# Keys and values of a second memory layer: from fillers inside a recurrent mixer to four joints between phases

## The reference, cut to what matters

```
def memory_cross_attention(h, mem, mem_kv_norm, mem_w_q, mem_w_kv, mem_w_o):
    q = (h @ mem_w_q)                       # 512 tokens, 4 heads of 128
    kv = rms_norm_2(mem, mem_kv_norm) @ mem_w_kv   # 256 tokens, 512 keys and 512 values
    k, v = kv[..., :512], kv[..., 512:]
    return block_attention(q, k, v, MEM_DIM ** -0.5) @ mem_w_o
```

## Time and profile before

| | us |
|---|---|
| median of three runs | 3618.82 (3618.14 to 3618.84) |
| the profiled execution | 3619.59 |
| its span on the core | 3617.6 |
| TensorE busy | 3500.1 (97%) |
| VectorE busy | 1948.1 (54%) |
| ScalarE busy | 1442.4 (40%) |
| mean granted TensorE clock | 0.992 |

### The profile page before, as it was taken

The page is one execution under the profiler, slowest core; times in us unless marked ns, Lnnn a source line. Parts: engine busy times, 40 slices in busy tenths (PEclk is TensorE's granted clock), DMA queues, the critical chain, the costliest instruction groups (busy, mean ns, idle before and its releaser), DMA issues.

```text
span 3617.6 us, 54110 instructions
## 1 busy us (share of the span) xinstructions
PE 3500.1 (97%) x21350; PEld 2891.6 (80%) x21350; DVE 1948.1 (54%) x2680; ACT 1442.4 (40%) x2153; POOL 29.3 (1%) x51
## 2 busy tenths in 40 slices
PE   8999998999999999999899999999999999999998
PEld 7888776768887888899678888877888897778887
DVE  4443489554434443335854433574777338567753
ACT  3333433143323332334643333573544236544432
POOL 0000000000000000000000000000000000000000
PEclk9999999999999999999999999999999999999999
DMA  3233222212232223322013233202232330123332
GB/s 129 97 105 107 93 71 82 75 64 98 93 97 83 94 98 95 92 82 89 23 59 98 95 96 93 66 13 70 82 99 96 94 107 18 47 70 99 99 95 92
DMA packets 85457, 303.41 MB, mean 84 GB/s; under 512 B 9712, under 2 KB 9712, under 8 KB 84400
## 3 DMA queue, kind: packets, MB, share of 16 engines
q1 hardware_dynamic: 82512, 288.24, 25.2%
q0 software_dynamic: 2784, 12.85, 1.0%
HBM read 294.76 MB, written 6.29 MB: 83 GB/s over the span
## 4 chain that ended last, share of the span: by engine, by line
PE 90%; DVE 6%; ACT 2%; issue 1%; DMA 0%; SPq 0%; DVEq 0%; ACTq 0%
PE PS L255 23%; PE PS L246 22%; PE PS L247 22%; PE PS L355 2%; PE PS L352 2%; PE PS L353 2%; PE PS L1065 2%; PE PS L1089 1%; PE PS L1076 1%; PE PS L386 1%; PE PS L2258 1%; DVE H_LO L479 1%; PE PS L2262 1%; ACT WHI L218 1%; DVE WLO L222 1%
## 5 line engine op out<-in xcount | busy, mean ns | idle before, releaser
L246 PE MATMUL PS<-WK_R,WHI 128*128 128x512 f32 x3648 | 1429.6, 392 | 16.8 <-DVE WLO L222 7.6
L247 PE MATMUL PS<-WK_R,WLO 128*128 128x512 f32 x3648 | 1423.7, 390 | 0.0
L222 DVE TENSOR_TENSOR WLO<-RAW,WHI 128x1024 fp32r<-128x1024 f32 x547 | 669.6, 1225 | 1150.1 <-ACT WHI L218 1147.4
L218 ACT ACTIVATE WHI<-RAW 128x1024 fp32r<-128x1024 f32 x547 | 579.4, 1059 | 998.6 <-PE PS L255 843.4
L246 PEld LDWEIGHTS PS<-WK_R,WHI 128*128 128x128 f32 x3648 | 687.5, 188 | 170.0 <-issue 22.3
L247 PEld LDWEIGHTS PS<-WK_R,WLO 128*128 128x128 f32 x3648 | 687.7, 189 | 142.6 <-issue 0.7
L255 PE MATMUL PS<-H_LO,WHI 128*128 128x512 f32 x2680 | 671.6, 391 | 3.9 <-DVE H_LO L479 3.9
L255 PEld LDWEIGHTS PS<-H_LO,WHI 128*128 128x128 f32 x2680 | 502.2, 188 | 115.9 <-DVE H_LO L479 13.1
L255 PE MATMUL PS<-HID_LO,WHI 128*128 128x512 f32 x1056 | 263.2, 389 | 0.0
L255 PEld LDWEIGHTS PS<-HID_LO,WHI 128*128 128x128 f32 x1056 | 197.9, 188 | 40.9
L1257 DVE SCALAR_TENSOR_TENSOR SC<-SC,VEC 128x511 f32<-128x511 f32 x176 | 132.2, 751 | 110.5 <-ACT SC L1224 98.6
(11 more groups left out here) (377 smaller groups left out, 3479.3 us busy)
## 6 DMA issues: line engine op xcount, KB each, us to landing
RAW<-in_ffn_gu SPq DMA_DIRECT2D x176, 512.0 KB, 3.5
RAW<-in_f_up SPq DMA_DIRECT2D x88, 512.0 KB, 3.6
RAW<-in_ffn_dn SPq DMA_DIRECT2D x64, 512.0 KB, 3.5
RAW<-in_c_in SPq DMA_DIRECT2D x32, 512.0 KB, 3.5
RAW<-in_f_dn SPq DMA_DIRECT2D x32, 512.0 KB, 3.6
RAW<-in_ffn_dn SPq DMA_DIRECT2D x32, 384.0 KB, 3.1
RAW<-in_a_in SPq DMA_DIRECT2D x22, 512.0 KB, 3.5
RAW<-in_m_qk SPq DMA_DIRECT2D x16, 512.0 KB, 3.6
```

The lines of the kernel that those rows point to most:

```text
L218: nc.scalar.activation(WHI[:, slot, :], RAW[:, slot, :], ACT.Copy).then_inc(S("w_hi"), 1)
L222: nc.vector.tensor_tensor(WLO[:, slot, :], RAW[:, slot, :], WHI[:, slot, :].bitcast(F32), ALU.subtract).then_inc(S("w_lo"), 1)
L246: pe.matmul(o, WHI[:, slot, w], hi(k), start=(first and b_ == 0), stop=False)
L247: pe.matmul(o, WLO[:, slot, w], hi(k), start=False, stop=False)
```

## The change: what it does

The 64 units of layer 1 leave mixa: `FILL` counts are about halved (the six between the first and the second token products become none), with their eight weight loads, four group copies, four stores and one 1 MB load of `memn_kept[1]`. At each of the four joints behind a ffn, the three products without use are replaced by one group of 16 units (`joint_pe`), copied by ScalarE (`joint_act`) into HID's last tile and stored by POOL (`joint_store`). From the second joint on, POOL first reads back `memn_kept[1]` (1 MB) at the start of the down product; at every joint it loads two weight pieces of 512 KB. VectorE waits for the joint's products before it writes H_LO, and for the store to have landed before it goes on into the next phase.

```diff
@@ norm_spread
             pe.wait_ge(S("norm_recip"), n + 1)
+            if n - 1 in joints:
+                pe.wait_ge(S("joint_copied"), joints[n - 1] + 1)
@@ norm_act
+            if pos - 1 in joints:
+                joint_act(act, joints[pos - 1], joint_bank(pos - 1))
             if not late(pos):
                 norm_root(act, n, P0)
@@ new
+        joint_memn = mem_raw
+        joint_kept = HID[:, FT - 1, :]
+        def joint_pool(pool, n, b):
+            pool.wait_ge(S("piece_done"), b["N"] + 2 * FT)
+            pool.dma_start(flat(H, 0, DT * MEM), memn_dram[1]).then_inc(S("joint_loaded"), 16)
+            joint_load(pool, n)
+            joint_store(pool, n)
+        def joint_pe(pe, n, b_):
+            pe.wait_ge(S("joint_loaded"), 32 + 48 * n)
+            for u in range(16):
+                ...
+            mm.then_inc(S("joint_done"), 1)
+        def joint_act(act, n, b_):
+            act.wait_ge(S("joint_done"), n + 1)
+            nc.scalar.activation(joint_kept, PS[:, b_, :], ACT.Copy).then_inc(S("joint_copied"), 1)
@@ post_pe
-            for _ in range(3):
-                pe.matmul(PS[:, 4 * last.slot + 3, :], ident, con("reset"), start=True, stop=True)
+            if kind == "ffn":
+                pos = [p for p in joints if plan[p][3]["post"] == m][0]
+                joint_pe(pe, joints[pos], joint_bank(pos))
+            else:
+                for _ in range(3):
+                    pe.matmul(PS[:, 4 * last.slot + 3, :], ident, con("reset"), start=True, stop=True)
@@ VectorE, each phase
+                if pos - 1 in joints:
+                    dve.wait_ge(S("joint_done"), joints[pos - 1] + 1)
                 norm_dve(dve, b["norm"], input_gain(kind, idx))
+                if pos - 1 in joints:
+                    dve.wait_ge(S("joint_stored"), 16 * (joints[pos - 1] + 1))
@@ mixa, FILL: units behind each step
-            FILL["gram", kind, par] = 4        # four places
+            FILL["gram", kind, par] = 3
-            FILL[kind, q] = 2                  # n, w, z: twelve places
+            FILL[kind, q] = 1
-        FILL["f", half] = 4                    # two places
+        FILL["f", half] = 2
-            FILL["e", half, k] = 4             # four places
+            FILL["e", half, k] = 2
-            FILL["tokens", k, x] = 2           # twelve places
+            FILL["tokens", k, x] = 1
-            FILL["rho",] = 6
+            FILL["rho",] = 0
-        FILL["state", c] = 2                   # fifteen places
+        FILL["state", c] = 1
-    FILL["last",] = 4
+    FILL["last",] = 1
-    assert total == 128
+    assert total == 64
```

More of the change, by code:

```diff
@@ L529, in build, with joint_weights, joint_load, joint_store @@
         kv_dram = nc.dram_tensor("kv_kept", (2, 128, 4 * T), F32, kind="Internal").ap()
+        joint_memn = mem_raw
+        joint_kept = HID[:, FT - 1, :]
+        joints = {pos: n for pos, (kind, _, n, _) in enumerate(plan) if kind == "ffn"}
+        def joint_weights(i):
+            return flat(H, 4 + 2 * i, PIECE)
+        def joint_load(pool, n):
+            for i in range(2):
+                w = dram["m_qk"][1, 4 + 2 * n + i] if n < 2 else dram["m_v"][1, n - 2, :, PIECE * i:PIECE * i + PIECE]
+                pool.dma_start(joint_weights(i), w).then_inc(S("joint_loaded"), 16)
+        def joint_store(pool, n):
+            pool.wait_ge(S("joint_copied"), n + 1)
+            if n < 2:
+                pool.dma_start(kv_dram[1, :, T * n:T * n + T], joint_kept).then_inc(S("joint_stored"), 16)
+            else:
+                d = kv_dram[1, :, 2 * T:4 * T].rearrange("p (b v) -> p b v", b=2)[:, :, 256 * (n - 2):256 * (n - 2) + 256]
+                pool.dma_start(d, joint_kept.rearrange("p (b c) -> p b c", b=2)).then_inc(S("joint_stored"), 16)
         def mem_pool(pool):
@@ L533, in mem_pool, with joint_bank @@
             pool.dma_start(mem_raw, dram["m_mem"]).then_inc(S("mem_loaded"), 16)
-            for l, planes in enumerate((mem_squares, mem_raw)):
-                pool.wait_ge(S("memn_made"), DT * (l + 1))
-                pool.dma_start(memn_dram[l], planes.rearrange("p k t -> p (k t)")).then_inc(S("memn_stored"), 16)
+            pool.wait_ge(S("memn_made"), DT)
+            pool.dma_start(memn_dram[0], flat(H, 4, DT * MEM)).then_inc(S("memn_stored"), 16)
+            pool.wait_ge(S("memn_stored"), 16)
+            joint_load(pool, 0)
+            pool.wait_ge(S("memn_made"), 2 * DT)
+            pool.dma_start(memn_dram[1], flat(H, 0, DT * MEM)).then_inc(S("memn_stored"), 16)
+            joint_store(pool, 0)
+        def joint_pool(pool, n, b):
[5 more added lines that the diff above has]
+            pe.wait_ge(S("joint_loaded"), 32 + 48 * n)
+            if n == 0:
+                pe.wait_ge(S("memn_made"), 2 * DT)
+            for u in range(16):
+                i, k = u // 8, u % 8
+                w = joint_weights(i)
+                if n < 2:
+                    mm = pe.matmul(PS[:, b_, 256 * i:256 * i + 256], w[:, 128 * k:128 * k + 128], joint_memn[:, k, :], start=(k == 0), stop=(k == DT - 1))
+                else:
+                    t, d = k // 4, 4 * i + k % 4
+                    mm = pe.matmul(PS[:, b_, 256 * t:256 * t + 256], joint_memn[:, d, 128 * t:128 * t + 128], w[:, 256 * (k % 4):256 * (k % 4) + 256],
+                                   start=(u == 0), stop=(u == 15))
+            mm.then_inc(S("joint_done"), 1)
+        def joint_act(act, n, b_):
+            act.wait_ge(S("joint_done"), n + 1)
+            nc.scalar.activation(joint_kept, PS[:, b_, :], ACT.Copy).then_inc(S("joint_copied"), 1)
+        def joint_bank(pos):
+            kind, _, _, b = plan[pos]
+            return 4 * out_panel(group(b, kind, 1), DT - 1).slot + 1
         def mem_sum_bank(where):
@@ L825, in _ @@
                     mem_pool(pool)
+                elif pos in joints:
+                    joint_pool(pool, joints[pos], b)
                 if kind != "ffn" and "pool" in mods[kind]:
@@ L1295, in pool @@
     def pool(pool, idx, n, b):
-        pool.wait_ge(S("kv_stored0"), 16 * 4)
-        pool.wait_ge(S("kv_stored1"), 16 * 4)
+        if idx == 0:
+            pool.wait_ge(S("kv_stored0"), 16 * 2)
+            pool.wait_ge(S("kv_stored1"), 16 * 2)
+        else:
+            pool.wait_ge(S("joint_stored"), 16 * 4)
         pool.wait_ge(S("norm_squares"), DT * (b["norm"] + 1))
@@ L2179, in sp @@
         dram = env["dram"]
-        for i in range(16):
-            l, k, slot = i // 8, i % 8, (out[1] + i) % 2
+        for k in range(8):
+            i, slot = k, (out[1] + k) % 2
             if i < 2:
@@ L2185, in sp @@
                 sp.wait_ge(S("kv_used"), i - 1)
-            w = dram["m_qk"][l, 4 + k] if k < 4 else dram["m_v"][l, (k - 4) // 2, :, PIECE * (k % 2):PIECE * (k % 2) + PIECE]
+            w = dram["m_qk"][0, 4 + k] if k < 4 else dram["m_v"][0, (k - 4) // 2, :, PIECE * (k % 2):PIECE * (k % 2) + PIECE]
             sp.dma_start(env["RAW"][:, slot, :], w).then_inc(S(f"kv_loaded{slot}"), 16)
-        sp.wait_ge(S("kv_used"), 16)
+        sp.wait_ge(S("kv_used"), 8)
         load(sp, out, lambda e, s_: env["dram"]["a_out"][e], 2, DT - 2)
@@ L2201, in pool @@
         pool.dma_start(flat(HID, 8, DT * MEM), env["memn_dram"][0]).then_inc(S("mem_loaded"), 16)
-        for g in range(8):
-            if g == 2:
-                pool.wait_ge(S("inverse"), 1)
-                pool.wait_ge(S("wy_done"), 4)
-                pool.dma_start(flat(HID, 16, DT * MEM), env["memn_dram"][1]).then_inc(S("mem_loaded"), 16)
+        for g in range(4):
             pool.wait_ge(S("kv_copied"), g + 1)
-            l, k = g // 4, g % 4
+            l, k = 0, g
             if k < 2:
@@ L2245, in kv_unit @@
         def kv_unit(u):
-            l, piece, k = u // 64, u // 8, u % 8
-            slot, w, x = (N_out + piece) % 2, env["RAW"], memn[l]
+            piece, k = u // 8, u % 8
+            slot, w, x = (N_out + piece) % 2, env["RAW"], memn[0]
             if u == 0:
                 pe.wait_ge(S("mats_masked"), 4)
-            if u % 64 == 0:
-                pe.wait_ge(S("mem_loaded"), 32 + 16 * l)
+                pe.wait_ge(S("mem_loaded"), 32)
             if k == 0:
```

11 lines of the change are left out of this document (6 added, 5 removed).

## The result

The changed kernel takes 3641.7 us (median of 6 runs, 3637.7 to 3642.9) against 3618.8 for the kernel before (6 runs, 3616.0 to 3622.4): ratio 1.0057, 95% interval 1.0047 to 1.0067. The forecast was 3617 with a range to 3627. The profiled execution took 3641.43, its span is 3639.6, 22.0 more than before, and the mean granted clock 0.981 (before 0.992).

A forecast was written before the change was run, and what follows sets the result against it. The prediction took TensorE to bound the kernel, in mixa limited by instructions arriving in blocks of 128 records. Joints +15.0 and mixa -16.4 sum to -1.4 us, giving 3617 us, range 3606 to 3627.

The forecast's parts named there:

- The state step should stay at 2.1 us with TensorE idle in it: Mixa's state loop: VectorE's 2.11 us sets the step, while TensorE's falls from 2.11 to about 1.58 us.
- the main case: Products moved one for one, instruction supply taking what fillers gave back: 3617 us, own range 3612 to 3622, chance 0.52.
- the rival that it falls: Granted clock falls to half in mixa's state loop: 1.0 us a step, 14 us in all, 3631 us; chance 0.14.
- nine of the fourteen steps: Clock rival in the state loop: from this many steps at half clock on, the kernel is over 0.2% slower.
- gaps and all: Argument against the clock rival: all three stretches of the n to token steps before the change kept clock 1.00.
- Supply of instructions: Mixa's n steps to state loop: instructions arrive in blocks of 128 records, 3.75 us each, 69.8 us for 18.6 blocks.
- some 5 and 5: VectorE's waits in mixa, 16.77 us for the token products and 6.04 for the first state step, should shrink to these.
- Mixa in all: Gain of the thinned mixa: 13.5 us ahead of the state loop plus 2.9 behind it, 16.4 us.
- The joints: Cost of 16 units replacing three products at four joints: 4.7 + 0.7 + 4.8 + 4.8 = 15.0 us.
- the cover: Before ffn 2 TensorE waits for VectorE at each tile and can catch up, so that joint costs only 0.7 us.
- the hidden wait for the store: Before ffn 2: store lands at 1171.9, VectorE's split could begin at 1172.2, so the wait is hidden by 0.3 us.
- The sum: Whole kernel: joints' cost 15.0 less mixa's gain 16.4 gives -1.4 us.

The follow-up runs named there:

- loop_thinned: Kernel before, with one of the two units of each of the 15 state steps left out, no joints; 3618.6 us, ratio 0.9997.
- gap_filled: Changed kernel with six empty products (they add zeros) in the bare place behind the first four token steps; 3617.5 us, ratio 0.9996.
- late_tokens_filled: Changed kernel with an empty product beside the units of the last eight token steps only; 3619.3 us, ratio 0.9999.
- gap_wait: Changed kernel with TensorE waiting in the bare place for VectorE's second addition instead of its first, no product added; 3641.5 us, ratio 1.0062.
- joints_alone: Kernel before with the four joints added, mixa keeping all 128 units and its stores; 3637.0 us, ratio 1.0049.
- units_moved: Changed kernel with six real units moved from the n, w and z steps into the bare place; 3640.9 us, ratio 1.0059.
- loop_filled: Changed kernel with one more product beside each unit of the 15 state steps; 3621.8 us, ratio 1.0011.
- concentrated: Changed kernel with its 64 units placed otherwise: none in n to e steps, two per token step, an empty product per state step; 3623.9 us, ratio 1.0008.
- tokens_filled: Changed kernel with an empty product beside each unit of the twelve token steps, state loop left thin; 3618.3 us, ratio 1.0001.
- gap_two: Changed kernel with two empty products in the bare place instead of gap_filled's six; 3621.5 us, ratio 1.0011.
- mixa_alone: Changed kernel without its joints: mixa keeps 64 units, the three products of before stand behind the feed-forward layers; 3629.6 us, ratio 1.0030.
- loop_bare: Kernel before with 24 of the state loop's 30 units left out; 3623.8 us, ratio 1.0015.

## Why the prediction was wrong, step by step

**The step that failed** is "The state step should stay at 2.1 us with TensorE idle in it": the main case takes it that the thinned stage keeps the full clock, and gives the rival that it falls a chance of 0.14 and no place in the range. Measured, the step is 3.00 us and TensorE is busy through all of the loop. The rival had the mechanism and most of the size: 1.0 us a step foreseen, 3.00 - 2.03 measured, 3631 forecast. It placed the cause wrong: the thinned loop holds its clock (loop_thinned), while the thinned token steps with the bare place in them lose it (gap_filled, late_tokens_filled, gap_wait), and the changed kernel's loop doesn't regain it. What exactly in these steps lets it fall stays open (joints_alone, units_moved). So it was not "nine of the fourteen steps" but all, with half the token steps and the stage behind the loop too. From gap_filled to the changed kernel the stage mixa differs by 8.95 + 10.11 = 19.1 us, and the medians by 24.

The argument against the rival was that three stretches of before kept 1.00, "gaps and all". But those stretches held two or more full-size units in each step, and the window that I took as the hardest case (1.55 of 3.40 us busy) was a pause inside them. Before the change no row showed the clock under thin steps over a long stretch. Near as it lay, I should have weighed that as unknown, and not as evidence.

The clock, fallen at 652.0 in loop_filled, came back in the filled loop at 665.7, and in the changed kernel's loop it did not, though TensorE was busy 42.00 of 42.00 us there. The Trainium skill ("TensorE: Matmul & The Clock Gate", section What's actually happening) says that activity releases the slow clock. loop_filled agrees with it; the changed kernel's loop, busy throughout by the profile, doesn't show it.

**Supply of instructions.** Right, with a block 0.1 us too short. Gaps at each 128th record, 3.67 us a packet; the n to state stretch took 74.8 us with the clock already falling in it, and 71.9 in gap_filled, against 69.8 forecast (3.75 us a block; 3.9 measured there). The concentrated run shows it without cover. The sentence of the Trainium skill that instruction streams are moved when the program is loaded ("Trainium Architecture — The Big Picture", section The software stack) is not what these traces show: 16 packets of that kind moved in 58.7 us of the run.

**VectorE.** Its waits of 16.77 and 6.04 us became 9.61 and 5.66, not some 5 and 5. The second holds the slow clock too; with the clock held (gap_filled) they are 9.64 and 2.95, 12.6 in all, since the blocks came later than forecast. Its step is 2.03 us and not 2.11; the rest was TensorE's, which had been busy through the whole loop.

**Mixa in all.** With the clock held it gives 14.3 us in gap_filled (10.11 + 4.2 for the joint), 14.5 in tokens_filled, 14.9 in late_tokens_filled, 17.5 in gap_two: around the 16.4 forecast. These kernels hold products that the forecast kernel lacks, so none of them is its mixa.

**The joints.** Forecast 4.7 + 0.7 + 4.8 + 4.8 = 15.0; measured 4.2 + 0.36 + 4.2 + 4.3 = 13.1. The 3.65 us of eight units held the end of the last one, which overlaps with what follows; in the joint 16 units took 6.72, 0.42 each and not 0.46. That before ffn 2 the cover holds was right, and so was the hidden wait for the store: no idle time of VectorE for `joint_stored` is noted there. The store landed after 2.7 us and not the 5.0 that the prediction priced, at about 1178, and VectorE's split began at 1180.2, so it is hidden by some 2 us and not by 0.3.

**Mixc.** The stage lost 8.50 us, of which 4.2 are the joint; the other 4.3 are not in the prediction. The clock is at half for 20 us in this stage instead of 10. It is no effect of the joint alone, since mixa_alone has it without one (4.26), loop_bare too (4.3), and joints_alone doesn't have it with one. Why it falls there in some kernels is open.

**The sum.** -1.4 was forecast. With the clock held, gap_filled shows -14.3 + 4.2 + 0.36 + 5.62 + 5.40 = +1.3 for the same stages. The median of that kernel lies 0.9 us below before all the same; differences of this size are within the interval.

## What to carry to other kernels

A filler can be worth its place twice: once in the result that it computes, and once in the clock that it helps to hold for the small products around it. Before fillers are thinned or moved, look in windows at what full-size work stays between the small products, over the whole stretch and not only in the loop that one is afraid for; after it, read the granted clock of each stretch first. A few products without use in the barest place can be the cheapest repair: here six gave 24 us back. They hold TensorE for 2.77 us, but the token steps got only 0.3 us longer than with two (23.94 against 23.68), since TensorE would have waited there in any case. It is a repair and no gain: 3617.5 is the time of before. And it has to be tried and not assumed, since six real units in the same place, taken from the steps ahead, gave nothing back.

## What the runs showed of the hardware that was not expected

The clock that a thin loop runs at depends on what came ahead of it: the same 482 records took 42.0 us or 28.1.

Busy time doesn't tell when the clock falls: in the state loop of loop_thinned TensorE idled 12% (3.3 of 28.1 us) and kept it, in the changed kernel it idled 13% (1.36 of 10.20 us) ahead of the fall and lost it. Nor does it tell when the clock comes back: the changed kernel's loop was busy 42.00 of 42.00 us and stayed at half.

Transfers slow the supply of instructions: 75.5 us instead of 81.9 for the same 2476 records when what the DMA moved in that stretch fell from 7.1 to 3.7 MB.

At the edge one program shows two times, 3614 to 3622 and 3635 to 3640 in gap_two, with mean clocks of 0.989 to 0.992 and 0.982 to 0.984. A median of such a kernel describes neither.
